# Six reorderings of the vector and scalar queues in a four-layer fp32 transformer kernel

## The reference, cut to what matters

```python
def dilated_mixer(x, w_in, w_out, cos, sin):      # sparse attention, three patterns
    h = x @ w_in                                   # 2048 x 20480
    ...                                            # rope, three windowed attentions, merged by their lse
    y = o.reshape(B, S, DSA_WIDTH).astype(x.dtype) * jax.nn.silu(z)
    return y @ w_out
def mla_mixer(x, w_in, q_norm, w_uq, kv_norm, w_ukv, w_out, cos, sin): ...
for layer in range(DEPTH):                         # one layer of each mixer
    x = layer_norm(DEEPNORM_ALPHA * x + y, ln_g[layer], ln_b[layer])
for l in range(DEPTH):                             # then two layers of the second block
    shift, scale, gate = jnp.split(c_act @ w_ada[l] + b_ada[l], 3, axis=-1)
    h = rms_norm_2(x, norm_w[l]) * (1.0 + scale[:, None, :]) + shift[:, None, :]
    ...                                            # h @ w_in[l]; gated linear attention (GLA), gated delta
    ...                                            # rule (GDN) and differential attention (DIFF)
    y = jnp.concatenate([o_gla, o_gdn, o_diff], axis=-1) @ w_out[l]
    x = x + gate[:, None, :] * y
```

## Time and profile before

| what | us |
|---|---|
| median of three runs | 2605.23 |
| the profiled execution | 2602.41 |
| its span | 2600.6 |
| PE busy | 2539.0 (98%) |
| DVE busy | 1967.2 (76%) |
| ACT busy | 1223.4 (47%) |
| mean granted TensorE clock | 0.997 of full |

### The profile page before, as it was taken

One profiled execution on the slowest core, in us unless ns is written; L12 is line 12 of the kernel. 1 busy time (PEld: TensorE's weight loads), 2 busy tenths in 40 slices (PEclk: granted clock), 3 DMA queues, 4 the chain that ended last, 5 costly groups with the idle time before them and its releaser, 6 DMA issues.

```text
span 2600.6 us, 33996 instructions
## 1 busy us (share of the span) xinstructions
PE 2539.0 (98%) x12919; PEld 2138.9 (82%) x12919; DVE 1967.2 (76%) x3325; ACT 1223.4 (47%) x1799; POOL 15.1 (1%) x32
## 2 busy tenths in 40 slices
PE   8999999999999999999999979999999999999999
PEld 6888888888888887878888869888887798888787
DVE  6898988998889987665555657677886567668865
ACT  4444444444443444445555456443445564433453
POOL 0000000000000000000000000000000000000000
PEclk9999999999999999999999999999999999999999
DMA  7787777877778776545445545444445544444444
GB/s 284 264 292 267 282 258 262 296 269 284 244 273 300 263 271 226 198 158 168 135 135 178 178 112 165 131 145 130 130 162 171 166 150 147 138 137 146 146 148 144
DMA packets 266018, 516.98 MB, mean 199 GB/s; under 512 B 16576, under 2 KB 20992, under 8 KB 265216
## 3 DMA queue, kind: packets, MB, share of 16 engines
q1 hardware_dynamic: 264256, 508.43, 57.1%
q0 software_dynamic: 1600, 6.38, 1.0%
HBM read 512.68 MB, written 2.10 MB: 198 GB/s over the span
## 4 chain that ended last, share of the span: by engine, by line
PE 84%; DVE 11%; ACT 3%; issue 3%; DMA 0%; DVEq 0%; SPq 0%; ACTq 0%
PE proj L562 14%; PE proj L564 14%; PE proj L563 14%; PE proj L1179 7%; PE proj L1181 7%; PE proj L1180 7%; PE scores L680 3%; DVE w_lo L1752 2%; DVE arena L1878 2%; PE proj L593 1%; PE proj L1171 1%; PE proj L1173 1%; PE proj L1174 1%; PE proj L594 1%; PE proj L595 1%
## 5 line engine op out<-in xcount | busy, mean ns | idle before, releaser
L1752 DVE TENSOR_TENSOR w_lo<-w_raw,w_hi 128x1024 fp32r<-128x1024 f32 (+1 forms) x744 | 900.2, 1218 | 302.7 <-ACT w_hi L1218 242.5
L1218 ACT ACTIVATE w_hi<-w_raw 128x1024 fp32r<-128x1024 f32 (+1 forms) x744 | 776.8, 1052 | 687.7 <-PE proj L564 377.2
L562 PE MATMUL proj<-w_hi,xt_lo 128*128 128x512 f32 x1632 | 652.0, 399 | 7.0 <-DVE xt_lo L1766 6.9
L564 PE MATMUL proj<-w_hi,xt_hi 128*128 128x512 f32 x1632 | 638.6, 391 | 0.0
L563 PE MATMUL proj<-w_lo,xt_hi 128*128 128x512 f32 x1632 | 637.6, 391 | 0.0
L1179 PE MATMUL proj<-w_hi,xt_lo 128*128 128x512 f32 x976 | 396.1, 406 | 4.3 <-DVE w_lo L1752 4.0
L1181 PE MATMUL proj<-w_hi,xt_hi 128*128 128x512 f32 x976 | 381.0, 390 | 0.0
L1180 PE MATMUL proj<-w_lo,xt_hi 128*128 128x512 f32 x976 | 380.5, 390 | 0.0
L562 PEld LDWEIGHTS proj<-w_hi,xt_lo 128*128 128x128 f32 x1632 | 308.0, 189 | 70.2 <-DVE xt_lo L1766 8.6
L564 PEld LDWEIGHTS proj<-w_hi,xt_hi 128*128 128x128 f32 x1632 | 307.4, 188 | 66.0
L563 PEld LDWEIGHTS proj<-w_lo,xt_hi 128*128 128x128 f32 x1632 | 308.2, 189 | 60.5
(11 more groups left out here) (385 smaller groups left out, 2902.8 us busy)
## 6 DMA issues: line engine op xcount, KB each, us to landing
w_raw<-in_dsa_w_in_dram SPq DMA_DIRECT2D x159, 1024.0 KB, 7.4
w_raw<-in_w_in_dram SPq DMA_DIRECT2D x120, 1024.0 KB, 5.1
arena<-in_w_ada_dram SPq DMA_DIRECT2D x192, 512.0 KB, 5.9
w_raw<-in_w_out_dram SPq DMA_DIRECT2D x32, 1024.0 KB, 5.1
w_raw<-in_mla_w_in_dram SPq DMA_DIRECT2D x24, 1024.0 KB, 5.2
w_raw<-in_dsa_w_out_dram SPq DMA_DIRECT2D x16, 1024.0 KB, 5.1
w_raw<-in_mla_w_out_dram SPq DMA_DIRECT2D x16, 1024.0 KB, 5.1
w_raw<-in_mla_w_ukv_dram SPq DMA_DIRECT2D x8, 1024.0 KB, 5.3
```

What stands on the lines that cost most here:

```text
L562: mm(o, xt[1][:, k0 + kk, tok], WH[:, c % 2, k, 0:n], start=first, stop=False)
L564: ins = mm(o, xt[0][:, k0 + kk, tok], WH[:, c % 2, k, 0:n], start=False, stop=last)
L1218: A(hi[:, 2 * q:2 * q + 2, 0:n], RAW[:, c % 4, 2 * q:2 * q + 2, 0:n], ACT.Copy).then_inc(hi_made, 1)
L1752: V.tensor_tensor(lo[:, ks, 0:n], RAW[:, c % 4, ks, 0:n], hi[:, ks, 0:n].bitcast(F32), ALU.subtract).then_inc(lo_made, 1)
```

## The change

Six edits, all of order:

1. Start: DVE's `tables_of()` goes from iteration 5 to iteration 6, behind low half 6 and the lo parts of group 2. (The tuple in `lo_in` holds the same numbers as `X_AT`.)
2. Sparse attention: the first six y turns go from slots 314 to 319 to slots 315, 317, 318, 319, 320, 321, on PE, ACT and DVE alike.
3. Seam to MLA, ACT: a square root of one column is made ahead of the seam, into scratch space. `hi_x(0)` and `hi_x(1)` go ahead of rounds 9 and 10, `hi_x(2)` ahead of round 13.
4. Seam to MLA, DVE: low half 11 goes ahead of the residual and statistics of the second tokens.
5. GLA, both layers: `gla_keys` is signalled ahead of the clearing of `SBD`.
6. Squares later: in both layers DVE's last `squares` and root argument go behind the lo parts of turn group 0. In the seam to the last layer ACT's `square_last(1)` goes behind round 10 and `affine(2)`.

```diff
+Y_TURNS = (3, 5, 6, 7, 8, 9, 17, 17)
...
-                        yield last + (2 * g + t + 2 if g < 3 else 17)
+                        yield last + Y_TURNS[2 * g + t]
...
+            own(A(AR[:, 768:769], ONES[:, 0:1], ACT.Sqrt))
+
...
             round_in(C_MLA_IN, 6)
             root(small[:, 16:17])
-            for h in range(7, 11):
+            round_in(C_MLA_IN, 7)
+            round_in(C_MLA_IN, 8)
+            hi_x(0)
+            round_in(C_MLA_IN, 9)
+            hi_x(1)
+            for h in range(10, 13):
                 round_in(C_MLA_IN, h)
-            hi_x(0)
-            round_in(C_MLA_IN, 11)
-            hi_x(1)
-            round_in(C_MLA_IN, 12)
+            hi_x(2)
             round_in(C_MLA_IN, 13)
-            hi_x(2)
             hi_x(3)
...
                     round_in(c1, 9)
-                    square_last(1)
                     round_in(c1, 10)
                     affine(l + 1, 2)
+                    square_last(1)
                     root(small[:, 19:20])
...
-                if h in X_AT:
-                    lo_in(X_AT.index(h))
+                if h in (0, 3, 6, 8):
+                    lo_in((0, 3, 6, 8).index(h))
...
-                if h == 5:
+                if h == 6:
                     tables_of()
...
             low_in(C_MLA_IN, 10)
+            low_in(C_MLA_IN, 11)
             last_block(0, C_DSA_OUT, B_DSA_OUT + 3, 1)
-            low_in(C_MLA_IN, 11)
             lo_x(3)
...
+                own.sync()
+                dve.sem_inc(S("gla_keys"), 1)
                 own(V.memset(SBD, 0.0))
                 own.sync()
-                dve.sem_inc(S("gla_keys"), 1)
...
-                    yield (AT_SPREAD - 1, AT_TURNS[0])[p]
-                    squares(u4, SUM[:, 0:4], SQD.rearrange("p (a n) -> p a n", a=4))
-                    own.sync()
-                    root_arg(256.0, RMS_EPS, SUM)
+                    def out_squares():
+
+                        squares(u4, SUM[:, 0:4], SQD.rearrange("p (a n) -> p a n", a=4))
+                        own.sync()
+                        root_arg(256.0, RMS_EPS, SUM)
+
+                    if p == 0:
+                        yield AT_SPREAD - 1
+                        out_squares()
...
+                    if g == 0:
+                        out_squares()
```

## The result

The changed kernel takes 2589.46 us, the median of five runs (2588.32 to 2589.72). Five runs of the kernel before on the same chip have the median 2604.70 (2601.54 to 2609.01). The ratio is 0.9941, with a 95% interval of 0.9927 to 0.9956: the change saves between 11.5 and 19 us. The forecast was 2589.3.

What follows compares the result with a forecast made beforehand. PE, busy 98% of the span, was taken as the bound, so only its standing time, 61.6 us, could be won. Terms 4.4 + 5.4 + 1.9 + 0.2 + 0.8 + 3.2 = 15.9 off 2605.2 gave 2589.3 us, range 2582 to 2598.

Steps and rivals of the forecast that it cites:

- the main case: Whole kernel: the six edits' gains add to 15.9 us, giving 2589.3 us; chance 0.73.
- the give-back of 0.2 us: Start: the moved tables delay the lo parts of group 3 to 34.4, where PE arrives at about 34.2.
- The lower bound of 3.2: Start, moved tables: gain in us if the clock stays low, with only half 4's earlier start won.
- the upper bound: Y turns in sparse attention: 6.3 us gained if a small second wait goes too.
- turn 5 does not hold half 324: Y turns: turn 5 was to be late next, its lo part at 1033.2 and half 324 at 1034.5.
- the load's 1.28 us: Seam to MLA: the dummy root takes the table load off DVE's path, so its chain starts 1.28 us earlier.
- The bound "0": GLA keys signalled ahead of the clearing: least gain 0, most 1.6 us in each layer.
- DVE takes nothing back: Rival: DVE's 48 us stretch does not start earlier, so moving the tables gives nothing net; 2593.7 us, chance 0.08.
- The clock did fall in a seam: Rival: waits left in the seams lower the clock, 1.4 us at each of three places; 2593.6 us, chance 0.08.
- The load does not stay: Rival: the table load stays ahead of the root, the seam to MLA gives 0.6 us; 2590.6 us, chance 0.04.
- Edit 5 does not pay in full: Rival, GLA: signalling keys early pays in full, DVE's chain being shorter by 1.4 us; 2586.5 us, chance 0.04.
- The slower rival, 24 column sums: Sparse attention: PE waits 0.8 us for each of 24 DVE sums, partly at lower clock; 48 us, 2637, chance 0.03.

Runs made afterwards that it cites:

- after_no_e1: Changed kernel with DVE's tables_of() put back from iteration 6 to iteration 5; 2593.92 us.
- after_again: Changed kernel once more, same instructions in the same order, two source lines written otherwise; 2588.98 us, ratio to the kernel before 0.9946.
- e12: Kernel before with only tables_of() moved to iteration 6 and the new slots of the y turns; 2594.0 us, ratio 0.9957.
- e5_no_clear: As e5_keys, but the clearing of SBD cut to one column, so part of the computation is left out; 2602.23 us.
- clear_on_pool: Changed kernel with the clearing of SBD moved from DVE to GpSimd, DVE waiting for it only ahead of the first state; 2585.52 us.
- e5_keys: Kernel before with only gla_keys signalled ahead of the clearing of SBD, with one more own.sync(); 2604.41 us.

## Why the prediction was right, and where only its sum was

The number was met, 2589.3 against 2589.46, and the main case happened. The forecast was 15.9 us less than a median of 2605.2; the medians of five differ by 15.2. Its terms did not all come out.

| term | forecast | bounds | measured |
|---|---|---|---|
| edit 1 | 4.4 | 3.2 to 4.6 | 2.7 in most executions; 5.0 in the profile of before, 6.1 in after_no_e1 |
| edit 2 | 5.4 | 3.9 to 6.3 | 6.1 |
| edits 3 and 4 | 1.9 | 0.6 to 2.6 | 2.0 with the clock up, 0.4 and 1.3 in two profiles, 1.67 alone |
| edit 5, both layers | 0.2 | 0 to 3.2 | -0.56 |
| edit 6a, both layers | 0.8 | 0 to 4.8 | 0.94 |
| edit 6b | 3.2 | 1.5 to 3.5 | 3.0 |
| sum | 15.9 | | 14.2 |

The measured column adds to 14.2 us with edit 1 at 2.7 and edits 3 and 4 at 2.0. The medians differ by 15.2, and by 13.5 beside after_again (2602.5 against 2588.98); 14.2 lies between. So the agreement to 0.2 us is chance: edits 1 and 5 gave 2.5 us less than forecast, and edit 2 gave 0.7 more. The base had luck in it too: all 22 runs of the kernel before on record have the median 2603.2, 2 us under the 2605.2 that I started from.

- **Edit 1.** The mechanism was right: half 4 starts at 27.19 without a wait, forecast 27.65, and the give-back of 0.2 us is not to be seen. The step that failed took the profiled start for the usual one. The clock went to its upper level late in it, behind half 0, which has nothing to do with the tables. This made DVE 1.2 us late, and the longer wait that followed brought the clock down in half 4. In the seven profiles without this the wait is 2.3 to 3.0 us, not 3.5, and half 4 runs at full clock. The lower bound of 3.2 does not hold.
- **Edit 2.** Too small by 0.7. Besides the 3.92 us and the clock at the turn and the half (1.5), a second wait of 0.37 us at a later turn went, which I had put only into the upper bound. All five later turns start without a wait, and turn 5 does not hold half 324. The other 0.3 us I can't place in one row.
- **Edits 3 and 4.** Right in size while the clock holds, and edit 4 alone is worth nothing, as the prediction said. The waits came at 1.90, 1.12 and 0.98 us in after_again, forecast 2.2, 1.4 and 1.0. Within the term I split wrongly: the load's 1.28 us gave only 0.75 by themselves. The reordering, for which I had 0.6, gave 0.9 with a dip of the clock in it, and 1.3 in after_again (2.0 less 0.75).
- **Edit 5.** The direction of the argument was right: the wait is gone at L1064, and 1.5 us stand at slot 98, where they were forecast. The sign was wrong, since I costed what moved and not the second `own.sync()` that the diff adds (0.11 us), nor the 0.35 us in layer 0. The bound "0" came from there being no reason for a loss; the added instruction was one.
- **Edit 6a.** 0.47 in each layer, forecast 0.4. Turn group 1 waits 0.3 us and half 131 waits 1.58, forecast 1.8:

```profile
1955.10 1.16 PE L1132 MATMUL turn<-constants,y 128*128 128x128 f32 x8 [0.30 <-DVE xt_lo L2763]
...
1963.31 0.50 PE L1182 MATMUL proj<-w_hi,xt_lo 128*128 128x512 f32 x1 [1.58 <-DVE w_lo L1758]
```

- **Edit 6b.** 3.0 us, forecast 3.2, and steady.

**The rivals.** DVE takes nothing back from edits 1 and 2 (e12). The clock did fall in a seam, and near the price that the rival had named (1.4 us): 1.6 us in the first profile of after. But it fell in the kernel before too, at the start of the profiled execution and in the unedited seam of several others, so most of it widens the spread of both kernels instead of moving their difference. Only in the single pair of profiles does it matter: 1.7 us in the seam to layer 0 and 1.6 in the seam to MLA went against the change, and 2.4 at the start (5.06 against 2.7) for it. The row that the rival rests on was read too simply: the clock did not fall behind the wait of 2.16 us at 1521.74. It was at 1.00 up to 1518.70 and at 0.50 from 1518.80, ahead of that wait and behind one of 2.18 us at 1517.59. The load does not stay (it starts at 1089.97; with the 11.2 us that edits 1 and 2 saved ahead of it, this is 1101 on the clock of before, as forecast). Edit 5 does not pay in full, and e5_no_clear names the condition under which it would; clear_on_pool meets it, with 1.6 us in each layer. The slower rival, 24 column sums, did not come at all: the same two wait, 1.5 us together.

**What stays open.** In layer 0 edit 5 costs 0.36 us more than in layer 1. The trace of after shows there one idle time of 0.50 us on DVE at 1831.21, ahead of a low half, 0.35 longer than at the same place in layer 1, and e5_keys has the same two idle times. What ends them was not tested. Nor was it tried what decides whether the clock falls behind a given wait, and whether edit 2 makes the lower clock in the seam to layer 0 likelier.

## What to carry to other kernels

A wait that is removed from an engine which another engine drives pays only what that other engine's queue gets shorter; if the work stays in the same queue, look for the wait at the next place where the two meet, and count each synchronisation that the new order adds. Work that can go to an idle engine (here a clearing, to GpSimd) can pay what moving it about in the queue does not. And before a long wait in one profile is priced, see in the rows ahead of it whether an accident of that execution (here a clock that rose late, 15 us earlier) is in it; a second execution of the same kernel tells.

## What the hardware showed that was not expected

The same code at the same wait, to a hundredth of a microsecond, was followed by the full clock in one execution and by the lower level in another: 1.90 us of wait, then clock 1.00 or 0.50 over the next 5 us, and 1.6 us of difference at the end of the seam. An unedited seam took 51.25 to 54.95 us; one group of twelve matmuls in it took 1.69 or 3.19 us, with nothing between. In one start the clock was up at 14.43 us and in another not before half 0 had ended at 16.22, and by way of ACT's copy of a turn this reached DVE as 1.2 us. GpSimd cleared 128x1536 in 1.38 us, nearly as fast as DVE (1.34), and did not slow DVE's copy beside it. Single executions of the kernel before lie up to 9.5 us apart (2599.91 to 2609.44), so their differences say little of an edit here. The time between the same two matmuls does, in stretches where the clock stayed at 1.00: in the nine stretches that no edit touches it repeats to 0.2 us over the fourteen profiles, with one exception (966.38 us in after_no_e1, 966.7 elsewhere).
